# The two gates of a linear recurrence: four 128x128 block-diagonal products each, or 64-row products in pairs into two banks

## The reference

```
xblk = xc.reshape(bsz, t, 8, 64)                                  # xc: convolved input, 512 wide
r = sigmoid(einsum('btnc,ncd->btnd', xblk, w_r).reshape(...) + b_r)
i = sigmoid(einsum('btnc,ncd->btnd', xblk, w_i).reshape(...) + b_i)
log_a = -8 * r * softplus(-lam);  a = exp(log_a)
b = sqrt(-expm1(2 * log_a)) * (i * xc)
h_t = a_t * h_(t-1) + b_t                                         # then times gelu(gb), and a norm
```

## Time and profile before

| | |
|---|---|
| profiled execution | 3241.06 us, of which span 3239.4 us |
| median of the runs | 3241.18 us |
| TensorE busy | 2992.6 us, 92% of the span |
| VectorE / ScalarE / GpSimd busy | 79% / 62% / 30% |
| mixer steps in their steady state | from about 400 us to 2200 us |
| length of one steady step | about 64.4 us |

### The profile page before, as it was taken

How to read it: one execution, slowest core, us unless ns; L and a number is a source line. 1 busy time by engine, 2 the same in 40 slices (tenths; PEclk the granted TensorE clock), 3 DMA queues, 4 the chain that set the end, 5 groups by cost and what they waited for, 6 DMA issues and landing times. The chain is left out here.

```text
span 3239.4 us, 81774 instructions
## 1 busy us (share of the span) xinstructions
PE 2992.6 (92%) x28690; PEld 2240.4 (69%) x28691; DVE 2561.8 (79%) x7166; ACT 2006.8 (62%) x4447; POOL 956.3 (30%) x994
## 2 busy tenths in 40 slices
PE   5888999999999999999999999998699999999960
PEld 5777788878887888888788878885344555555530
DVE  6787788878887888788878878886788888888845
ACT  7555565666666665666565656553577777777746
POOL 4322222122212221222122212221344444544420
PEclk8899999999999999999999999998899999999985
DMA  6110122111111112121211121115387877677749
GB/s 227 60 34 17 58 86 73 67 67 67 67 66 66 68 66 68 66 72 62 75 63 67 66 74 60 67 60 202 116 258 220 245 204 217 187 220 221 224 101 391
DMA packets 117810, 380.28 MB, mean 117 GB/s; under 512 B 18560, under 2 KB 18688, under 8 KB 105216
## 3 DMA queue, kind: packets, MB, share of 16 engines
q1 hardware_dynamic: 82528, 269.96, 23.1%
q0 software_dynamic: 29216, 89.30, 12.1%
q10 hardware_dynamic: 5760, 16.85, 1.3%
HBM read 280.05 MB, written 96.01 MB: 116 GB/s over the span
## 5 line engine op out<-in xcount | busy, mean ns | idle before, releaser
L597 PE MATMUL pj<-uT,W 128*128 128x128 f16 x15744 | 980.3, 220 | 10.4 <-POOL W L1889 10.4
L597 PEld LDWEIGHTS pj<-uT,W 128*128 128x128 f16 x15744 | 934.4, 99 | 57.5 <-issue 47.5
L2247 DVE SCALAR_TENSOR_TENSOR W<-W,ecol 128x512 f16<-128x512 f16 x664 | 447.4, 746 | 107.0 <-ACT W L2191 107.0
L2191 ACT ACTIVATE W<-W,ecol 128x512 f16 x664 | 415.9, 709 | 79.3 <-issue 78.0
L2155 PE MATMUL bA<-W,uT 128*128 128x512 f16 x1992 | 447.0, 381 | 5.6 <-issue 4.4
L2155 PEld LDWEIGHTS bA<-W,uT 128*128 128x128 f16 x1992 | 193.6, 98 | 228.6 <-issue 9.6
L1950 POOL TENSOR_TENSOR dec<-tri,g 128x512 f32<-128x512 f32 x33 | 34.4, 1041 | 910.6 <-DVE g L1680 910.6
L2139 PE MATMUL pj<-W,qs 128*128 x664 | 300.4, 595 | 1.8 <-ACT qs L2218 0.9
L992 ACT ACTIVATE ht<-ht 128x512 f32<-128x512 f32 x256 | 159.8, 625 | 87.5 <-DMA ht<-w_up 82.2
L2139 PEld LDWEIGHTS pj<-W,qs 128*128 128x128 f32 x664 | 120.3, 191 | 122.1 <-issue 121.6
L1022 ACT ACTIVATE qh<-bA 128x256 f32<-128x256 f32 x198 | 76.8, 388 | 190.9 <-PE bA L763 186.9
(11 more groups left out here) (504 smaller groups left out, 6326.5 us busy)
## 6 DMA issues: line engine op xcount, KB each, us to landing
ht<-w_gate SPq DMA_DIRECT2D x128, 256.0 KB, 3.1
ht<-w_up SPq DMA_DIRECT2D x128, 256.0 KB, 3.2
W<-w_gate SPq DMA_DIRECT2D x32, 1024.0 KB, 5.0
W<-w_up SPq DMA_DIRECT2D x32, 1024.0 KB, 7.8
W<-w_down SPq DMA_DIRECT2D x32, 1024.0 KB, 12.1
x_in<-xm SPq DMA_DIRECT2D x33, 512.0 KB, 4.6
ht<-xm SPq DMA_DIRECT2D x32, 512.0 KB, 3.7
h_rows<-ht SPq DMA_DIRECT2D x32, 512.0 KB, 2.6
```

Source lines behind the costliest of these rows:

```text
L597: mm = pe.matmul(pj[g % 2][:, j, :], w16[:, k, w_half(w_high, COL[GROUPS[g]], 512, j * P, P)], (ul if low_u else uh)[:, k, :], start=(k == ...
L2191: nc.scalar.activation(part_of(wx[par][:, 0], k), raw[:, k], ACT.Copy, scale=ecol[par][:, k:k + 1]).then_inc(sem("wx_high"), 1)
L2247: a = nc.vector.scalar_tensor_tensor(out=part_of(wx[par][:, 1], k), in0=raw[:, k], scalar=ecol[par][:, k:k + 1], in1=part_of(wx[par][:, 0] ...
```

## The change

One array `gbd` takes the place of the two: for each j it has 128 rows and 128 columns, all of them weights. Rows 0 to 63 hold the r block in columns 0 to 63 and the i block in columns 64 to 127; rows 64 to 127 hold them the other way round (i, then r). A product of 64 rows (one half of the channels) gives both gates of that half: the lower half into bC, the upper half into bT, four j each. The r values then lie in bC partitions 0 to 63 and bT partitions 64 to 127, the i values in the other halves. ScalarE takes each with a sigmoid of 64 partitions: eight for r and eight for i, sixteen in a row. All eight products stand at the place of the former gate i, all sixteen sigmoids at that of the former i sigmoids; the four transposes into bT (L887) wait for i_gate as well.

```diff
-        wr_bd = sb("wr_bd", [P, 4, P])
-        wi_bd = sb("wi_bd", [P, 4, P])
+        gbd = sb("gbd", [P, 4, P])
...
-                nc.gpsimd.memset(wr_bd[:], 0.0)
-                nc.gpsimd.memset(wi_bd[:], 0.0)
...
+        halves = (slice(0, HALF), slice(HALF, P))
...
-                def gate(bd, done):
+                def gates():
 
                     for j in range(4):
-                        mm = pe.matmul(bC[:, j, :], bd[:, j, :], xc[:, j, :], start=True, stop=True)
-                    mm.then_inc(sem(done), 1)
+                        for bank, half in zip((bC, bT), halves):
+                            mm = pe.matmul(bank[:, j, :], gbd[half, j, :], xc[half, j, :], start=True, stop=True)
+                    mm.then_inc(sem("gi_full"), 1)
...
                     level_x(s, 4)
-                    if s.P:
-                        need(pe, sem("conv"), 16 * s.pP + 4)
-                        need(pe, sem("R_ready"), s.nG)
-                        for j in range(4):
-                            mm = pe.matmul(bC[:, j, :], wr_bd[:, j, :], xc[:, j, :], start=True, stop=True)
-                        mm.then_inc(sem("gr_full"), 1)
                     project(s, 3, 0)
                     level_y(s, 5)
                     project(s, 3, 1)
                     level_x(s, 5)
                     if s.P:
-                        need(pe, sem("r_gate"), s.nP)
-                        for j in range(4):
-                            mm = pe.matmul(bC[:, j, :], wi_bd[:, j, :], xc[:, j, :], start=True, stop=True)
-                        mm.then_inc(sem("gi_full"), 1)
+                        need(pe, sem("conv"), 16 * s.pP + 4)
+                        need(pe, sem("R_ready"), s.nG)
+                        need(pe, sem("yd_ready"), s.nO)
+                        need(pe, sem("kd_ready"), s.nG)
+                        gates()
...
                         need(pe, sem("yd_ready"), s.nO)
+                        need(pe, sem("i_gate"), s.nP)
...
+                def r_gates():
+
+                    for j in range(4):
+                        for bank, half in zip((bC, bT), halves):
+                            a = nc.scalar.activation(la[half, j, :], bank[half, j, :], ACT.Sigmoid, bias=lcol[half, 1, j:j + 1])
+                    a.then_inc(sem("r_gate"), 1)
+
+                def i_gates():
+
+                    for j in range(4):
+                        for bank, half, other in zip((bC, bT), halves, halves[::-1]):
+                            a = nc.scalar.activation(gx[half, j, :], bank[other, j, :], ACT.Sigmoid, bias=lcol[half, 2, j:j + 1])
+                    a.then_inc(sem("i_gate"), 1)
...
-                        need(act, sem("gr_full"), s.nP)
-                        need(act, sem("a_step"), 2 * s.nG)
-                        for j in range(4):
-                            a = nc.scalar.activation(la[:, j, :], bC[:, j, :], ACT.Sigmoid, bias=lcol[:, 1, j:j + 1])
-                        a.then_inc(sem("r_gate"), 1)
...
                     if s.P:
                         need(act, sem("gi_full"), s.nP)
+                        need(act, sem("a_step"), 2 * s.nG)
+                        r_gates()
                         need(act, sem("h_scan"), s.nG)
-                        for j in range(4):
-                            a = nc.scalar.activation(gx[:, j, :], bC[:, j, :], ACT.Sigmoid, bias=lcol[:, 2, j:j + 1])
-                        a.then_inc(sem("i_gate"), 1)
+                        i_gates()
```

More of the change, by code:

```diff
@@ L485, in _ @@
                 sp.dma_start(wo, w_out.rearrange("(k p) n -> p k n", p=P)).then_inc(sem("w_out_in"), 16)
-                for dst, src in ((wr_bd, w_r), (wi_bd, w_i)):
+                for other, src in enumerate((w_r, w_i)):
                     pair = src.rearrange("(j b) c d -> b c j d", b=2)
                     for b in range(2):
-                        sp.dma_start(dst[64 * b:64 * b + 64, :, 64 * b:64 * b + 64], pair[b]).then_inc(sem("bd_in"), 16)
+                        c = HALF * (b ^ other)
+                        sp.dma_start(gbd[HALF * b:HALF * b + HALF, :, c:c + HALF], pair[b]).then_inc(sem("bd_in"), 16)
                 def raw_chunks(s):
@@ L741, in opening @@
                     pe.wait_ge(sem("conv"), 4)
-                    gate(wr_bd, "gr_full")
+                    gates()
                     project_ba(s)
-                    pe.wait_ge(sem("r_gate"), 1)
-                    gate(wi_bd, "gi_full")
                     turn_x(s)
@@ L1076, in opening @@
                     evac(s, 3, "v", early=True)
-                    act.wait_ge(sem("gr_full"), 1)
-                    for j in range(4):
-                        a = nc.scalar.activation(la[:, j, :], bC[:, j, :], ACT.Sigmoid, bias=lcol[:, 1, j:j + 1])
-                    a.then_inc(sem("r_gate"), 1)
+                    act.wait_ge(sem("gi_full"), 1)
+                    r_gates()
                     act.wait_ge(sem("idx_zeroed"), ZEROED)
@@ L1083, in opening @@
                     high_halves(5)
-                    act.wait_ge(sem("gi_full"), 1)
-                    for j in range(4):
-                        a = nc.scalar.activation(gx[:, j, :], bC[:, j, :], ACT.Sigmoid, bias=lcol[:, 2, j:j + 1])
-                    a.then_inc(sem("i_gate"), 1)
+                    i_gates()
                     act.wait_ge(sem("la_ready"), 1)
```

## The result

The changed kernel took 3444.72 us (median of four runs, 3439.55 to 3457.62), against 3241.11 us before (the median with a fourth run of it): a ratio of 1.063, 95% interval 1.0615 to 1.0653, 204 us slower. The range given was 3303 to 3362. The direction and the place were right; the time added is 204 us where 97 were forecast.

A forecast was written before the change was run, and what follows sets the result against it. TensorE, busy 92% of the span, was taken to bound the kernel, with 0.7 us in hand for level 6's copy. 3241 us plus 67 for that copy's lateness plus 30 for the clock gave 3338 us, range 3303 to 3362.

The forecast's parts named there:

- What bounds the kernel, and the place: Mixer step: TensorE bounds it; level 6's copy on ScalarE, 0.7 us in hand, comes late, delaying level 6 by 2.12 us.
- The products: Gate products on TensorE: lower and upper halves run side by side, 0.9 us less a step, bounds 0.9 and 0.
- The sigmoids: ScalarE ahead of level 6's copy: sixteen at 0.25 us each, bounds 0.12 and 0.25, eight more adding 2.0 us a step.
- The clock: TensorE behind each new 2.2 us gap: clock falls in two steps of three, 1.45 us each, 30 us, bounds 0 and 52.
- rival A: Steady steps: the gap is there but TensorE's clock stays up, 3308 us; chance 0.24.
- The sum: Whole kernel: 3241 us plus 67 for the late copy plus 30 for the clock, 3338 us.
- B: Gate products on TensorE: pairs don't run side by side, first sigmoid 0.35 us later, 3320 us; chance 0.08.
- C: TensorE behind each gap: clock stays low for long, two low stretches costing 3.1 us a step, 3404 us; chance 0.04.
- D: ScalarE: half-partition sigmoids so short that level 6's copy stays in time, 3212 us at best; chance 0.04.

The follow-up runs named there:

- e5: Changed kernel plus 36 unused float16 products on TensorE in the gap ahead of level 6's second product; 3375.12 us, ratio 1.0418.
- e4: Changed kernel's late place for both gates, but eight 128x128 products as in the kernel before and eight sigmoids on 128 partitions; 3265.99 us, ratio 1.0078.
- e6: Changed kernel's product pairs kept, but eight sigmoids on 128 partitions, half of each gate's values being the other gate's; 3242.2 us, ratio 1.0009.
- e8: Changed kernel plus 20 unused float16 products on TensorE ahead of level 6's second product, leaving 2.15 us idle; 3387.28 us.
- c1: Changed kernel's pairs moved behind level 4's second product, upper half into bO, sigmoids sorted by half and spread over ScalarE's idle stretches; 3228.04 us, ratio 0.9968.
- e3: Changed kernel with bC and bT read in turn, first eight sigmoids on the lower half, then eight on the upper; 3397.62 us.
- e1: Changed kernel with the sixteen sigmoids sorted: r from bC, r from bT, i from bC, i from bT, four each; 3387.15 us, ratio 1.0452.
- e7: Changed kernel with sigmoids ordered by half written: r lower, i lower, r upper, i upper; 3387.81 us.
- e2: Changed kernel with r read from bC only and i from bT only, lower and upper half in turn; 3430.94 us.

## Why the prediction was wrong, point by point

- **What bounds the kernel, and the place.** Right. The copy of level 6 became late, all TensorE work behind it moved with it, and no other wait mattered: with the gap filled (e5) a step is longer by 4.04 us, which is level 6's delay of 13.52 - 9.48 = 4.04 to the hundredth. The wait for i_gate at the transposes into bT cost nothing. One reading was wrong: "There is no gap between them." In the kernel before, the projection ahead of level 5's second product takes 1.34 us of the row like the others, to 1011.61, but that product starts at 1011.89, just behind ScalarE's copy (1011.84); the tail of the pipelined products counts as busy time and hides most of it. The forecast doesn't rest on it, since level 6's copy hangs on another chain.

```profile
1010.27 1.50 PE L597 MATMUL pj<-uT,W 128*128 128x128 f16 x24
1011.44 0.40 ACT L1022 ACTIVATE qh<-bA 128x256 f32<-128x256 f32 x1
```

- **The products.** Right in kind. The pairs run side by side, but the group takes 1090.15 - 1089.06 = 1.09 us of TensorE's row, not 0.89: the first pair stands 0.21 us ahead of the second, the last 0.20 ahead of the projection, the others 0.11. Level 5's second product ahead of them takes 0.60 us of the row; in e4, with 128-row products at the same place, it took 0.50. The saving is about 0.6 us, not 0.9 (e6: 0.58 us less busy a step), and the changed kernel doesn't see it, since it falls into the gap.
- **The sigmoids: the step that failed.** "Bounds 0.12 and 0.25", "above I see no reason for more". The price was carried over from four sigmoids on the same 128 partitions, which overlap; sixteen that change their half each time don't, and follow at 0.375 us. From the first sigmoid to the tanh, 4.01 us became 6.01. With it level 6 is at 13.5 instead of 11.6. The earlier trace rows held the right upper bound: a single sigmoid lasts 0.366 us, and 16 x 0.37 = 5.9 us is what a run without any overlap takes. The sum should have carried both.
- **The clock: mis-sized, and for the wrong reason.** The predicted term was 1.0 us a step for a gap of 2.2 us; at such a gap it is 0.19 (e8), and at the real gap of 4.3 us it is 2.25. A fall behind a stall like that of 2.06 us in the earlier trace rows came in 3 of 26 steps of e8, not in two of three. Had the sigmoids cost 0.25 us, then by an estimate from e8's 0.19 us a step the time would have been 3241 + 67 + 6 = 3314 us, nearer to rival A's 3308 than to 3338; no run has that kernel.
- **The sum.** 2.12 us predicted, 1.92 more from the spacing, 2.25 from the clock, together 6.29 us; times 32 it is 201 us. The two profiled executions are 198.6 us apart: 27.5 ahead of the 26 steps (five steps, so the opening itself cost nothing that shows), 163.6 in them, 7.5 behind. Of it 196 us lie in the mixer; the medians, 204 us apart, hold a few microseconds more that no run explains.
- **The rivals.** B (no side by side) is refuted by the pairs. C (the clock low for long) came nearer than its chance of 0.04: it priced two low stretches behind each gap, 3.1 us a step, and here 19 of 26 gaps had 6.8 us at 0.50, two of 3.4, which with the rest cost 2.25. But it set them behind a gap of 2.2 us, where e8 shows three falls of 3.4 us in 26 steps. D is refuted: half the partitions save nothing.

## What to carry to other kernels

Before cutting an instruction in two on the partitions, price the pieces at their full duration, not at the distance at which equal ones follow each other; the distance holds only while the half of the partitions read and the half written stay the same. Work saved on the busiest engine is worth nothing behind a copy that it waits for: first read how much time this copy has in hand (here 0.7 us) before putting eight instructions ahead of it. The same change with its pieces spread over the other engine's idle stretches (c1) gained 0.3% instead of losing 6%.

## What the runs showed of the hardware

ScalarE overlapped two sigmoids of 128 columns from PSUM only if both read the same half of the partitions and both wrote the same half (with the bias from the half written): 0.25 us apart, else 0.37 to 0.39. An activation on all partitions overlapped with one that writes the lower half, and not with one that writes the upper. Another PSUM bank in between doesn't matter (e3), nor does a crossing of halves inside one instruction (e1, e7), nor the number of partitions (four on 64 took 1.10 to 1.14 us, four on 128 took 1.13 to 1.16). TensorE's clock, after about 60 us of dense work in each step: after 1.40 us idle it never fell, after 2.15 us three times in the steady steps, after 2.88, 3.64 and 4.34 us each time, to 0.50. What makes it fall behind 2.15 us in some steps and not in others stays open. A group of 64-row pairs between 128-row products cost 0.2 us on top of its passes, and 0.1 us more in the row ahead of it.

One thing stays open. The expert part, the same in all but e2, e3 and e6, took between 955 us (before) and 968 us (e1) in the profiled executions, without order by what was changed in the mixer (after 958, c1 957, e4 967, e5 967). No run here looked for the cause; it limits what a total can tell of a few microseconds, and is why the steps are compared.
